# Splitting raw tiles ahead of their token factor beside the norms of a two-layer transformer block

## The reference, cut to what matters

```python
def rmsnorm(x, g):
    xf = x.astype(jnp.float32)
    y = xf * lax.rsqrt(jnp.mean(xf * xf, axis=-1, keepdims=True) + EPS)
    return (y * g.astype(jnp.float32)).astype(x.dtype)

for l in range(DEPTH):
    n = rmsnorm(h, attn_norm[l])
    proj = n @ w_in[l]                       # 1024 -> u, v_sgu, q, k, v_att, 512 each
    u = gelu(u); v_sgu = gelu(v_sgu)
    ...
    h = h + mixed @ w_out[l]
    h = h + conv_ffn(rmsnorm(h, ffn_norm[l]), w_up[l], conv_w[l], conv_b[l], w_down[l])
```

## Time and profile before

| what | value |
|---|---|
| median of 3 runs | 2048.31 us (2045.89 to 2048.55) |
| the profiled execution's own time | 2049.57 us |
| its span, first to last instruction | 2047.8 us |
| mean granted TensorE clock | 0.941 |
| busy: TensorE, VectorE, ScalarE, GpSimd | 1868.2, 1040.2, 765.2, 705.4 us |
| matmuls of TensorE | 8750 |

### The profile page before, as it was taken

The page is one execution under the profiler, slowest core; times in us unless marked ns, Lnnn a source line. Parts: engine busy times, 40 slices in busy tenths (PEclk is TensorE's granted clock), DMA queues, the critical chain, the costliest instruction groups (busy, mean ns, idle before and its releaser), DMA issues. The chain is left out here.

```text
span 2047.8 us, 24762 instructions
## 1 busy us (share of the span) xinstructions
PE 1868.2 (91%) x8750; PEld 1505.4 (74%) x8750; DVE 1040.2 (51%) x1782; ACT 765.2 (37%) x1219; POOL 705.4 (34%) x340
## 2 busy tenths in 40 slices
PE   5999989999998999899999996998787779999996
PEld 4777778888886867778888885887555558888875
DVE  6558555555546258555555446435664362222225
ACT  3434343333333334343333334445654232222231
POOL 2432234444533422234444442225100324444440
PEclk8999989999997999989999996979898879999997
DMA  6211214444323221214344322203101203223211
GB/s 225 82 76 48 72 49 156 133 143 133 114 81 123 83 82 42 72 62 143 133 143 136 137 81 78 75 14 119 42 1 42 82 0 124 82 93 112 82 41 41
DMA packets 102384, 183.42 MB, mean 90 GB/s; under 512 B 6650, under 2 KB 66604, under 8 KB 100268
## 3 DMA queue, kind: packets, MB, share of 16 engines
q1 hardware_dynamic: 101928, 181.74, 25.8%
q10 hardware_dynamic: 388, 0.79, 0.1%
HBM read 180.42 MB, written 2.10 MB: 89 GB/s over the span
## 5 line engine op out<-in xcount | busy, mean ns | idle before, releaser
L746 POOL TENSOR_TENSOR w_lo<-raw,w_hi 128x1024 fp32r<-128x1024 f32 (+1 forms) x331 | 703.0, 2129 | 1265.3 <-ACT w_hi L785 1265.0
L1782 PE MATMUL ps<-n_hi,w_hi 128*128 128x512 f32 x1408 | 564.8, 401 | 18.5 <-DVE n_lo L1203 15.0
L1783 PE MATMUL ps<-n_lo,w_hi 128*128 128x512 f32 x1408 | 555.0, 394 | 0.0
L1784 PE MATMUL ps<-n_hi,w_lo 128*128 128x512 f32 x1408 | 554.4, 394 | 0.0
L785 ACT ACTIVATE w_hi<-raw 128x1024 fp32r<-128x1024 f32 (+1 forms) x331 | 312.5, 946 | 320.0 <-PE ps L1784 222.2
L1782 PEld LDWEIGHTS ps<-n_hi,w_hi 128*128 128x128 f32 x1408 | 268.8, 191 | 80.9 <-issue 14.1
L1783 PEld LDWEIGHTS ps<-n_lo,w_hi 128*128 128x128 f32 x1408 | 268.8, 191 | 58.8 <-issue 3.6
L1784 PEld LDWEIGHTS ps<-n_hi,w_lo 128*128 128x128 f32 x1408 | 268.4, 191 | 57.5
L1782 PE MATMUL ps<-x_hi,w_hi 128*128 128x512 f32 x672 | 271.5, 404 | 8.9 <-DVE x_lo L1203 8.9
L1783 PE MATMUL ps<-x_lo,w_hi 128*128 128x512 f32 x672 | 268.6, 400 | 0.0
L1784 PE MATMUL ps<-x_hi,w_lo 128*128 128x512 f32 x672 | 268.2, 399 | 0.0
(11 more groups left out here) (247 smaller groups left out, 1939.6 us busy)
## 6 DMA issues: line engine op xcount, KB each, us to landing
raw<-in_w_up SPq DMA_DIRECT2D x44, 1024.0 KB, 7.2
raw<-in_w_ff SPq DMA_DIRECT2D x32, 1024.0 KB, 6.6
raw<-in_w_in SPq DMA_DIRECT2D x28, 1024.0 KB, 7.4
zb<-in_ada_w SPq DMA_DIRECT2D x16, 1536.0 KB, 8.3
raw<-in_w_down SPq DMA_DIRECT2D x44, 512.0 KB, 4.0
raw<-in_w_out SPq DMA_DIRECT2D x12, 1024.0 KB, 6.4
za<-in_x SPq DMA_DIRECT2D x1, 2048.0 KB, 9.9
raw<-in_cmp_w_k SPq DMA_DIRECT2D x2, 1024.0 KB, 6.8
```

Of the source, the lines that this page charges most:

```text
L746: pool.tensor_tensor(split_quarter(st.kind, w_lo, g % 4, q), raw_quarter(st.kind, raw[st.index % 2], q), split_quarter(st.kind, w_hi.bitca ...
L1782: pe.matmul(out, l_hi, r_hi, start=start, stop=False)
L1783: pe.matmul(out, l_hi, r_lo, start=False, stop=False)
L1784: return pe.matmul(out, l_lo, r_hi, start=False, stop=stop)
```

## The change

For the stage next to each norm of the first block (`vs` behind the attention norm, up group 0 behind the feed-forward norm), raw tiles are split: ScalarE rounds gain x h (`raw_hi`), VectorE makes gain x h less that (`raw_lo`). They lie in buffers that are free at the time (`raw_parts`). The products of this stage read them. The factor is applied to the results: as the scale of the values' gelu (tokens lie over the partitions there), and for up group 0 by VectorE's `first_scaled`, in place in the bank, before the convolution. For the feed-forward norm the factor is copied from PSUM to `sq`. TensorE makes the sums and the spread inside the stage: after quarter 1 and in quarter 2 of `vs` of layer 0; before `vs` and in its quarter 0 in layer 1; at steps k = 2 and k = 5 of up group 0. The `n_hi` and `n_lo` of the later stages are made as before, but behind the spread. Some `ensure` calls move.

```diff
+            def raw_hi(e, f, ready):
+                act.wait_ge(*ready)
+                act.activation(raw_parts(e, f)[0], h[:, f, :], ACT.Copy, scale=raw_gain(e, f)).then_inc(rawhi_ready, 1)
...
                 if l == 0:
+                    ensure(g0 + 1)
+                    emptied(act, "cols0")
+                    for f in range(DT):
+                        if f in (3, 5, 7):
+                            ensure(g0 + f // 2 + 1)
+                        raw_hi(("attn", 0), f, (free[f], BK["x", f][1] + 1))
                     squares(("attn", l), lambda f: h[:, f, :], lambda f: (free[f], BK["x", f][1] + 1))
+                ensure(g0 + 4)
                 root(("attn", l), D)
-                ensure(g0 + 4)
-                split_tiles(("attn", l), DT, 0)
+                for f in range(DT):
+                    if f in (2, 4, 6):
+                        ensure(g0 + 4 + f // 2)
+                    k = SPL["attn", l] + f
+                    split_hi(k, tb[:, k % 3, :], n_hi[:, f, :])
                 if l == 0:
                     tables()
-                ensure(g0 + 4 + LOOK)
+                act.wait_ge(rstd_ready, NRM["attn", l][0] + 1)
                 for t in range(NT):
-                    act.activation(vg[:, t, :], filled(act, ("vs", l, t))[:, :], ACT.Gelu_apprx_tanh)\
-                        .then_inc(freed(("vs", l, t)), 1)
+                    act.activation(vg[:, t, :], filled(act, ("vs", l, t))[:, :], ACT.Gelu_apprx_tanh,
+                                   scale=rstd[:, t:t + 1]).then_inc(freed(("vs", l, t)), 1)
...
                     ensure(STR["outa", l].g0 + m // 2 + LOOK + 1)
+                    raw_hi(("ffn", l), m, (freed(("outa", l, m)), BK["outa", l, m][1] + 1))
                     square(("ffn", l), m, h[:, m, :], (freed(("outa", l, m)), BK["outa", l, m][1] + 1))
+                ensure(STR["up", l, 0].g0 + 4)
                 root(("ffn", l), D)
...
                         for t in (2 * i, 2 * i + 1):
+                            if first and t == 0:
+                                ffn_hi(0)
+                                ffn_hi(1)
                             run_ahead(t)
-
-                            act.wait_ge(quarter_done, STR["up", l, 0].g0 + t + 1 if first else gq + t + 1 + 8 * (j - 1))
+                            if first:
+                                act.wait_ge(up_scaled, 4 * l + t + 1)
+                            else:
+                                act.wait_ge(quarter_done, gq + t + 1 + 8 * (j - 1))
...
+                        if first and i == 0:
+                            for f in range(2, DT):
+                                ffn_hi(f)
...
+            def raw_lo(e, f):
+                dve.wait_ge(rawhi_ready, RAW[e] + f + 1)
+                hi_, lo_ = raw_parts(e, f)
+                dve.scalar_tensor_tensor(lo_, h[:, f, :], raw_gain(e, f), hi_.bitcast(F32), ALU.mult, ALU.subtract)\
+                    .then_inc(rawlo_ready, 1)
...
                     if m:
+                        emptied(dve, ("outa", l, m - 1))
+                        raw_lo(("ffn", l), m - 1)
                         add_square(("ffn", l), m - 1)
...
+                def first_scaled(t):
+                    dve.wait_ge(quarter_done, STR["up", l, 0].g0 + t + 1)
+                    dve.tensor_tensor(ps[t][:, :], ps[t][:, :], factors, ALU.mult).then_inc(up_scaled, 1)
+
+                def beside_split(f):
+                    if f == 2:
+                        first_scaled(0)
+                        first_scaled(1)
+                    if f == DT - 1:
+                        first_scaled(2)
...
-                conv_steps(0)
+                conv_begin(0)
+                factors = sq[:, 0, :]
+                dve.tensor_copy(factors, norm_rstd(("ffn", l))).then_inc(freed(("rstd", ("ffn", l))), 1)
+                emptied(dve, ("rstd", ("ffn", l)))
+                norm_split(("ffn", l), ("ffn", l), DT, lambda f: h[:, f, :], lambda f: col("ffn_norm", l * DT + f), 0,
+                           beside=beside_split)
+                taps(0, 0)
+                taps(1, 0)
+                gate(0, 0)
+                first_scaled(3)
+                taps(2, 0)
+                taps(3, 0)
+                gate(1, 0)
...
+                def beside_values(q, t):
+                    if (q, t) == (1, NT - 1) and l == 0:
+                        norm_sums(("attn", l))
+                    if (q, t) == ((2, 1) if l == 0 else (0, 1)):
+                        spread(("attn", l))
...
+                    if raw is not None:
+                        ready(0)
+                        ready(1)
+                        for k in range(DT):
+                            pe.wait_ge(rawlo_ready, RAW[raw] + k + 1)
+                            one(0, k)
+                            one(1, k)
+                            if k == 2:
+                                norm_sums(raw)
+                            if k == 5:
+                                spread(raw)
```

More of the change, by code:

```diff
@@ L1316, in modulation @@
                 link(last)
+            for f in range(DT):
+                emptied(dve, ("x", f))
+                raw_lo(("attn", 0), f)
             for f in range(DT):
@@ new lines, in gate, with conv_steps @@
+                def gate(i, j):
+                    dve.wait_ge(free[2 * i + 1], n0[2 * i + 1] + j + 1)
+                    dve.wait_ge(silu_done, (l * FG + j) * 2 + i + 1)
+                    dve.tensor_tensor(rb[2 * i], rb[2 * i], rb[2 * i + 1], ALU.mult).then_inc(val_ready, 1)
+                def conv_steps(j):
+                    conv_begin(j)
+                    for i in range(2):
+                        taps(2 * i, j)
+                        taps(2 * i + 1, j)
+                        gate(i, j)
@@ L1848, in features, with raw_tokens, tokens @@
                     last.then_inc(quarter_done, 1)
-            def tokens(keys, g0, split=None):
+            def raw_tokens(keys, g0, e, beside):
+                outs = [bank(key) for key in keys]
+                for q in range(4):
+                    wh, wl = quarter(g0 + q)
+                    for k in (2 * q, 2 * q + 1):
+                        pe.wait_ge(rawlo_ready, RAW[e] + k + 1)
+                    for t in range(NT):
+                        for k in (2 * q, 2 * q + 1):
+                            c = (k % 2) * S
+                            x_h, x_l = (part[:, t * P:(t + 1) * P] for part in raw_parts(e, k))
+                            last = product(outs[t][:, :], x_h, x_l, wh[:, c:c + S], wl[:, c:c + S],
+                                           k == 0, k == DT - 1)
+                        if t == NT - 1:
+                            last.then_inc(quarter_done, 1)
+                        beside(q, t)
+            def tokens(keys, g0):
                 outs = [bank(key) for key in keys]
@@ L1856, in tokens @@
                         for k in (2 * q, 2 * q + 1):
-                            if split is not None and t == 0:
-                                pe.wait_ge(lo_ready, split + k + 1)
                             c = (k % 2) * S
@@ L2037, in _, with up @@
                     out_tile("outa", m, n_hi[:, HT:DT, :], n_lo[:, HT:DT, :])
-                norm_sum(("ffn", l))
                 n0 = BK.ffn[l]
-                def up(g, j, split=None):
+                def up(g, j, split=None, raw=None):
                     turn = 0 if isinstance(j, int) else 8 * (j - 1)
@@ L2051, in one @@
                         wh, wl = w_hi[:, (g + t) % 4, :], w_lo[:, (g + t) % 4, :]
+                        x_h, x_l = (n_hi[:, k, :], n_lo[:, k, :]) if raw is None else raw_parts(raw, k)
                         last = product(ps[t][:, :], wh[:, k * P:(k + 1) * P], wl[:, k * P:(k + 1) * P],
-                                       n_hi[:, k, :], n_lo[:, k, :], k == 0, k == DT - 1)
+                                       x_h, x_l, k == 0, k == DT - 1)
                         if k == DT - 1:
@@ L2063, in up @@
                             one(1, k)
-                    for t in range(0 if split is None else 2, 4):
+                    if raw is not None:
[9 more added lines that the diff above has]
+                                spread(raw)
+                    for t in range(0 if split is None and raw is None else 2, 4):
                         ready(t)
```

97 lines of the change are left out of this document (64 added, 33 removed).

## The result

The changed kernel takes 2063.16 us (median of 4 runs, 2060.07 to 2066.04) beside 2047.56 for the kernel before on the same chip: a ratio of 1.0084, 95% interval 1.0067 to 1.0101, so slower, by 0.8%. (The ratios here are those of the record; they differ a little from the quotients of the medians, here 1.0076.) In a second session it was 2063.12 beside 2048.52: 1.0076 (1.0049 to 1.0104). Forecast were 2061.7 us, from 2042 to 2070. The profiled execution of after took 2066.04 us (span 2064.2), 16.5 more than that of before.

A forecast was written before the change was run, and what follows sets the result against it. TensorE, busy for 91% of the span, was taken as the bound, with gains only in its waits around the norms. Start +7.1, feed-forward norms +4.4 and layer 1's attention norm +1.9 sum to 13.4: 2061.7 us, range 2042 to 2070.

The forecast's parts named there:

- The sum: Whole kernel: start 7.1, two feed-forward norms 4.4 and layer 1's attention norm 1.9 make 13.4 us slower.
- Start: Value and u stages of layer 0: u ends at 92.9, not 85.79, +7.1 us; bounds +2.3 and +8.4.
- a wait of 11.1: Layer 0's u stage: TensorE waits 11.1 us before the last 24 products, for u's last weight quarter.
- no stall at u's last quarter: Rival, layer 0's u stage: ScalarE reaches that quarter by 70, start -6.5 us, total 2048.1; chance 0.09.
- Feed-forward norms: Both first-block norms ahead of up group 0: +2.2 us each, +4.4 together; bounds -7.5 and +4.9.
- the wait for the sums: First up group: TensorE, in order, waits 2.8 us for the sums of squares although raw tiles are ready.
- the chain from the spread to the freed bank: First up group: VectorE's work behind the spread until bank 0 is free for the next group, 17.8 us.
- the wait ahead of the second group: Second up group: TensorE has 13.6 us of products during VectorE's chain and so waits 4.2 us.
- some 2.2 more for catches: Ahead of the feed-forward sums: VectorE operations on two SBUF tiles held up beside GpSimd's weight quarters, 2.2 us.
- the clock behind the wait for the sums: First up group: 18 products take 4.1 us, or 6.2 if the wait has brought TensorE's clock down.
- Attention norm of layer 1: Later sums move the value stage's start from 652.28 to 653.0, with the spread inside: +1.9 us; bounds -0.5 and +3.5.
- The raw tiles close the gaps: Rival, all first-block norms: GpSimd catches nothing, sums come at 261, together 24.5 us faster, 2024; chance 0.08.

The follow-up runs named there:

- before_again: The kernel before, unchanged, run once more for a second trace; 2054.55 us (one run).
- quarter_first: Against the changed kernel, ScalarE copies u's last weight quarter ahead of the sine and cosine tables in layer 0; 2064.66 us, 1.0074 to the kernel before.
- sums_late: Against the changed kernel, first up group makes the sums behind the last step of tiles 0 and 1, the spread in tile 2; 2061.26 us, 1.0054.
- no_up_lo: Against the changed kernel, GpSimd subtracts only 128 of 1024 columns per weight quarter of up group 0; 2050.83 us, 0.9989 to the kernel before.

## Why the prediction was right

**The sum** was 13.4 us; the medians say 15.6 and 14.6, and the terms as measured 14.8. That the numbers lie so near is in part luck. The two stretches for which the forecast had no term give back 5.3 us, so that at the last down group after stands at +9.5 against the first trace of before and at +13.4 against the second, and the second block adds its own part. Executions of the same kernel differ by more than sum and medians do.

**Start: +7.1 forecast, +7.2 measured** against the trace that the forecast used (up to +10.3 against before_again). Each station came: the end of the spread at 49.1 (48.60), the last subtraction's end at 64.5 (63.7), angles at 75.3 (74.4), gelus' end at 81.5 (81.15), a wait of 11.1 (10.94), u's end at 92.9 (93.00). Three n_lo were caught, as forecast. What the forecast had not seen is the second cause, hidden under the first: it priced the rival "no stall at u's last quarter" at 6.5 us better than before, and quarter_first shows that this gains nothing alone.

**Feed-forward norms: +2.2 each forecast, +3.2 and +3.1 measured.** The mechanism was right: the wait for the sums 2.8 (3.48), the chain from the spread to the freed bank 17.8 (17.4, from 280.45 to 297.85), the wait ahead of the second group 4.2 (3.39). Two terms were mis-sized. The smaller is "some 2.2 more for catches": four subtractions were caught, for 6.8 us in all (the excess over 0.75 of 2.38, 2.29, 2.31 and 2.82), each of GpSimd's four quarters meeting one, while the adds of squares lost nothing any more of the 3.5 us that they had lost before. That is 3.3 us more, and the sums were 9.0 us behind the last output product where 8.3 was forecast. The larger is the clock behind the wait for the sums: for the 18 products up to the spread the forecast took 4.1 us and named 6.2 as what the low clock would make of them, and they took 5.82:

```profile
273.58:279.40 5.82, 5.82 (x20) 4.59 (x20) 0.18 (x1) 0.26 (x1) 0.00 (x0) 0.71 0.39 150
```

So the spread ended 2.2 us later than the 272.6 that was taken (280.45, less the shift of 5.6), inside the 275.7 that the forecast allowed; the chain behind it and the clock behind the second wait gave back about 1 us.

**Attention norm of layer 1: +1.9 forecast, +1.3 measured** (+1.1 to +1.3 in six other traces, -0.1 in sums_late). The sums came 4.8 us later in the kernel's own time, where 5.8 was forecast.

**The rivals.** "The raw tiles close the gaps" needed sums without catches; no_up_lo, where GpSimd catches none, shows that even then the feed-forward norm gains 3.5 us and not 7.5, since VectorE's chain behind the spread stays.

## What to carry to other kernels

Work that is taken out of one engine's wait lands in another engine's queue; follow it there to everything that stands behind it, down to the small copies that free a bank. Three waits here ended with a short, unrelated item (a weight copy, a parameter copy, the modulation's sum) that stood behind the eight split tiles, and two of them came to light only when the wait above was gone. When two waits of one engine stand in a row, removing the first shows up in the second, so try them together.

## What the runs showed that I had not expected

The same instructions of the kernel before took 141.1 and 147.6 us in two executions, at a granted clock of 0.87 and 0.80; TensorE is busy there for 75 to 79% of the time, in short pieces.

GpSimd is held too. In the rows of after its quarter at 265.01 takes 3.04 us. When it began, a raw subtraction of VectorE was under way (264.43, two SBUF tiles), and the add of two SBUF tiles at 265.09 followed without a gap, up to 265.77; both took their usual time, 0.74 and 0.68. The quarter is longer by 0.63 than the one at 255.07 (2.41), which began beside an add with an operand in PSUM. The subtraction that came next (266.29) was the one to wait. In these rows, then, the work that was under way goes through whole and the other engine stands behind it, and what a quarter loses depends on how much of VectorE's work is left when it begins. The 0.3 that the prediction set against the rule of the Trainium skill ("SBUF — State Buffer", section "Who interferes with whom") was a mean over four quarters and such a value in between; these rows agree with the rule.
